# Rows of decays and gates over all partitions: transposing a column read with step 0, in place of a product with a diagonal matrix

## The reference

```python
# branch A, gated DeltaNet, 8 heads, both directions; per chunk, per head
G = cumsum(g)
decay = exp(where(tril, G[:, None] - G[None, :], -inf))
a_low = where(strict, (k*beta) @ k.T * decay, 0)          # unit triangular system
w_v, u_k = triangular_solve(a_low + I, [v*beta, k*beta*exp(G)])
v_new = w_v - u_k @ s
out   = (q*exp(G)) @ s + (q @ k.T * decay) @ v_new
s     = s*exp(G_last) + (k*exp(G_last - G)).T @ v_new

# branch B, mLSTM, 4 heads, both directions; per chunk, per head
d_log = where(tril, b[:, None] - b[None, :] + log_i[None, :], -inf)
m_t   = maximum(b + m, max(d_log, axis=-1))
p_ij  = exp(d_log - m_t[:, None]) * (q @ k.T)
num   = exp(b + m - m_t) * (q @ C) + p_ij @ v             # and den, C, n, m alike
```

## Time and profile before

| | |
|---|---|
| median of 3 runs | 3540.78 us (3540.35 to 3541.26) |
| profiled execution: span, first to last instruction | 3540.6 us |
| instructions profiled | 49,727 |
| TensorE busy | 3332.9 us (94%), 19752 matmul instructions |
| VectorE busy | 2341.5 us (66%) |
| ScalarE busy | 1778.2 us (50%) |
| GpSimd busy | 332.9 us (9%), 333 instructions |
| DeltaNet stage | about 1381 to 1737 us of the span |
| mLSTM stage | about 1737 to 1868 us of the span |

### The profile page before, as it was taken

One profiled execution on the slowest core, in us unless ns is written; L12 is line 12 of the kernel. 1 busy time (PEld: TensorE's weight loads), 2 busy tenths in 40 slices (PEclk: granted clock), 3 DMA queues, 4 the chain that ended last, 5 costly groups with the idle time before them and its releaser, 6 DMA issues. The chain is left out here.

```text
span 3540.6 us, 49727 instructions
## 1 busy us (share of the span) xinstructions
PE 3332.9 (94%) x19752; PEld 2737.8 (77%) x19752; DVE 2341.5 (66%) x2542; ACT 1778.2 (50%) x2276; POOL 332.9 (9%) x333
## 2 busy tenths in 40 slices
PE   5899999999999998999887999977999999999995
PEld 0799998989999998998767998865666666666663
DVE  1578557656665665455576334577888888888886
ACT  2444322333333333555555223445777777777774
POOL 0000000011100002322302100000100100010000
PEclk8999999999999999999998999998999999999997
DMA  9422324545555553112334434678999999999998
GB/s 413 153 93 90 143 108 134 177 165 188 182 175 183 179 171 107 37 49 58 118 85 153 157 109 152 251 274 304 376 390 396 394 379 397 395 376 397 397 376 319
DMA packets 181508, 796.78 MB, mean 225 GB/s; under 512 B 17508, under 2 KB 75236, under 8 KB 102116
## 3 DMA queue, kind: packets, MB, share of 16 engines
q1 hardware_dynamic: 163348, 702.44, 53.7%
q0 software_dynamic: 17136, 86.91, 7.4%
q10 hardware_dynamic: 864, 5.27, 0.4%
HBM read 732.10 MB, written 62.46 MB: 224 GB/s over the span
## 5 line engine op out<-in xcount | busy, mean ns | idle before, releaser
L2510 DVE TENSOR_TENSOR expert_lo<-expert_ring,first_expert_hi 128x2048 fp32r<-128x2048 f32 x288 | 660.1, 2292 | 111.8 <-ACT first_expert_hi L2447 108.0
L2447 ACT ACTIVATE first_expert_hi<-expert_ring 128x2048 fp32r<-128x2048 f32 x285 | 546.9, 1919 | 175.1 <-PE bank L2394 175.1
L2393 PE MATMUL bank<-expert_lo,xeT_hi 128*80 128x512 f32 x1024 | 402.0, 393 | 0.0
L468 PE MATMUL bank<-h_hi,part_hi 128*128 128x320 f32 x960 | 301.4, 314 | 8.2 <-DVE part_lo_x L856 4.5
L2392 PE MATMUL bank<-first_expert_hi,xeT_hi 128*80 128x512 f32 x768 | 303.2, 395 | 1.2 <-DVE xeT_lo L2515 1.2
L2394 PE MATMUL bank<-first_expert_hi,xeT_lo 128*80 128x512 f32 x768 | 299.1, 389 | 0.0
L468 PE MATMUL bank<-h_lo,part_hi 128*128 128x320 f32 x960 | 298.2, 311 | 0.0
L856 DVE TENSOR_TENSOR part_lo_x<-part_x,part_hi 128x1024 fp32r<-128x1024 f32 x120 | 149.4, 1245 | 152.5 <-ACT part_hi L680 145.3
L2510 DVE TENSOR_TENSOR expert_lo<-expert_ring,expert_hi 128x2048 fp32r<-128x2048 f32 x96 | 219.6, 2288 | 43.2 <-ACT expert_hi L2447 43.2
L680 ACT ACTIVATE part_hi<-part_x 128x1024 fp32r<-128x1024 f32 x120 | 127.3, 1061 | 217.2 <-PE bank L468 185.2
L468 PE MATMUL bank<-s_hi,part_hi 128*128 128x320 f32 x720 | 226.7, 315 | 3.7 <-DVE part_lo_x L856 3.7
(11 more groups left out here) (405 smaller groups left out, 7812.6 us busy)
## 6 DMA issues: line engine op xcount, KB each, us to landing
expert_ring<-d_wgate SPq DMA_DIRECT2D x128, 1024.0 KB, 7.0
expert_ring<-d_wup_e SPq DMA_DIRECT2D x128, 1024.0 KB, 7.6
expert_ring<-d_wdown SPq DMA_DIRECT2D x128, 1024.0 KB, 10.4
mod_slot<-d_wmod SPq DMA_DIRECT2D x56, 1024.0 KB, 6.9
part_b<-d_win SPq DMA_DIRECT2D x90, 512.0 KB, 3.7
front_ring<-d_wmod SPq DMA_DIRECT2D x40, 1024.0 KB, 8.0
front_ring<-d_win SPq DMA_DIRECT2D x29, 1024.0 KB, 5.0
d_proj<-out_rows POOLq DMA_DIRECT2D x86, 320.0 KB, 2.4
```

Of the source, the lines that this page charges most:

```text
L468: mm = pe.matmul(part_bank[j][:, 0:HALF_T], w, a[:, kk, :], start=(kk == 0 and x == 0), stop=(kk == HALF_K - 1 and x == 2))
L2393: pe.matmul(out[0:CAP, :], a_hi, lo, start=False, stop=False)
L2447: act.activation(w_hi[n % NSPLIT][:], w[:, n % NSLOT].rearrange("p (k n) -> p k n", n=HALF), ACT.Copy).then_inc(s["we_high"], 1)
L2510: dve.tensor_tensor(w_lo[n % NSPLIT][:], w[:, n % NSLOT].rearrange("p (k n) -> p k n", n=HALF), w_hi[n % NSPLIT][:].bitcast(F32), ALU.subt ...
```

## The change

A new function `rows_of_columns` takes the place of `add_mask` and of the product with ones. For each of the four heads TensorE transposes one column of G, ci or negM, which is read as 128 columns with step 0: a 128x128 operand whose columns are all the same, so that its transpose has the column as a row in every line. The transposition goes through the identity as k's and v's do, in 128 output columns per head. The mask's matmul comes after the four and adds onto them. The diagonal matrices are gone: diagG and diagC from GpSimd, diagM from VectorE, with their semaphores; TensorE now waits in the Mbc fill for negM itself (`nM`, raised by VectorE's drain before exp_neg_m), and in the G and Cbc fills for the bank only. Both hardware loops are written out: all five steps have constant waits and addresses on every engine.

```diff
-def add_mask(pe, k, bank, d):
-    pe.matmul(h4(bank[:]), k.ident_bf[:], all_heads(k.neg_bf[:, d, :]), start=True, stop=False)
+def rows_of_columns(pe, k, bank, columns4, d):
+    for h in range(4):
+        pe.matmul(bank[:, h * P:(h + 1) * P], columns4[:, h:h + 1].to_broadcast([P, P]), k.ident, start=(h == 0),
+                  stop=False, is_transpose=True, skip_group_check=True)
+    return pe.matmul(h4(bank[:]), k.ident_bf[:], all_heads(k.neg_bf[:, d, :]), start=False, stop=True,
+                     skip_group_check=True)
...
         def steps(eng, body):
-            body(0, (0, 0), 0)
-            with eng.Fori(0, TT - 1) as i:
-                body(i + 1, (i + 1, i * -1 + (TT - 1)), 1)
+            for step in range(TT):
+                body(step, (step, (TT - step) % TT), min(step, 1))
...
-                pool.wait_ge(bf, 3)
-                def diagonals(step, tiles, _):
-                    for q, d, h0 in QUADS:
-                        if not isinstance(step, int):
-                            A[q].wait_filled(pool, step + -1, "G")
-                        c = d * 8 + h0
-                        pool.tensor_tensor(dg[q][:], all_heads(k.ident), per_head(col(k.G[:], tiles[d], c, c + 4), P),
-                                           ALU.mult).then_inc(dg_ready[q], 1)
+                def strips_of(step, tiles, _):
                     for n in range(1, len(LEVELS)):
...
                     for q, d, h0 in QUADS:
-                        pe.wait_ge(dg_ready[q], step + 1)
                         A[q].wait_free(pe, step, "G")
-                        add_mask(pe, k, A[q].t, d)
-                        mm = pe.matmul(h4(A[q].t[:]), k.ones, dg[q][:], start=False, stop=True)
-                        mm.then_inc(A[q].filled, 1)
+                        c = d * 8 + h0
+                        rows_of_columns(pe, k, A[q].t, k.G[:, tiles[d], c:c + 4], d).then_inc(A[q].filled, 1)
...
# mLSTM: steps written out in the same way; GpSimd's body with diagC removed
-                        pe.wait_ge(s[d]["dgC"], step + 1)
                         b["D"].wait_free(pe, step, "Cbc")
-                        add_mask(pe, k, b["D"].t, 1 - d)
-                        pe.matmul(h4(b["D"].t[:]), k.ones, dg[d][:], start=False, stop=True).then_inc(b["D"].filled, 1)
+                        rows_of_columns(pe, k, b["D"].t, k.ci[:, tiles[d], 4 * d:4 * d + 4], 1 - d
+                                        ).then_inc(b["D"].filled, 1)
...
-                        pe.wait_ge(s[d]["dgM"], step + 1)
+                        pe.wait_ge(s[d]["nM"], step + 1)
                         b["D"].wait_free(pe, step, "Mbc")
-                        add_mask(pe, k, b["D"].t, d)
-                        pe.matmul(h4(b["D"].t[:]), k.ones, dgM[d][:], start=False, stop=True).then_inc(b["D"].filled, 1)
+                        rows_of_columns(pe, k, b["D"].t, nM[d][:], d).then_inc(b["D"].filled, 1)
...
-                        dve.drain()
+                        dve.drain().then_inc(s[d]["nM"], 1)
                         dve.tensor_scalar(enm[d][:], bM[d][:], -1.0, None, ALU.mult)
-                        dve.tensor_tensor(dgM[d][:], all_heads(k.ident), per_head(nM[d][:], P), ALU.mult
-                                          ).then_inc(s[d]["dgM"], 1)
```

More of the change, by code:

```diff
@@ L1008, in phase_deltanet @@
         staged = [sb(f"dn_staged{d}", [P, 24, P]) for d in range(2)]
-        ktok, vtok, dg, DT, sc = (quads(n) for n in ("ktok", "vtok", "diagG", "decayT", "scoresT"))
+        ktok, vtok, DT, sc = (quads(n) for n in ("ktok", "vtok", "decayT", "scoresT"))
         XT, R, vn, vs = (quads(n) for n in ("XT", "R", "vnew", "vweighted"))
@@ L1022, in phase_deltanet @@
                                                                        "dn_state_out"))
-        dg_ready = [k.sem(f"dg_ready{q}") for q in range(4)]
         QUADS = [(q, q % 2, 4 * (q // 2)) for q in range(4)]
@@ L1102, in diagonals @@
                             cut(pool, p, n).then_inc(strips[p], 1)
-                steps(pool, diagonals)
+                steps(pool, strips_of)
             @block.tensor
@@ L1376, in phase_mlstm @@
         staged2 = [dirs(f"ml_staged{b}_", [P, 16, P]) for b in range(2)]
-        ktok, dg, dgM, ET, PT, kw = (dirs(n, [P, 4, P]) for n in ("ml_ktok", "diagC", "diagM", "expT", "pT", "kweighted"))
+        ktok, ET, PT, kw = (dirs(n, [P, 4, P]) for n in ("ml_ktok", "expT", "pT", "kweighted"))
         vtok = dirs("ml_vtok", [P, 4, DA])
@@ L1387, in phase_mlstm @@
         landed2 = [[k.sem(f"ml_landed{b}_{d}") for d in range(2)] for b in range(2)]
-        sems = ("ready", "dgC", "dgM", "max", "expo", "scalars", "kw", "nu", "den")
+        sems = ("ready", "nM", "max", "expo", "scalars", "kw", "nu", "den")
         s = [{n: k.sem(f"ml_{n}{d}") for n in sems} for d in range(2)]
@@ L1395, in steps @@
         def steps(eng, body):
[L1396 to L1399, removed]
+            for step in range(TT):
+                body(step, (step, (TT - step) % TT), min(step, 1), step % 2, step // 2 + 1)
         def gate(t3, tiles, d, h=None):
@@ L1447, in _ @@
                 pool.drain().then_inc(o_zeroed, 1)
[L1449 to L1455, removed]
             @block.tensor
@@ L1525, in body @@
                         b["A"].wait_filled(act, step, "kT")
-                        if not isinstance(step, int):
-                            act.wait_ge(s[d]["kw"], step)
+                        wait(act, s[d]["kw"], step)
                         act.activation(ktok[d][:], h4(b["A"].t[:]), ACT.Copy).then_inc(b["A"].emptied, 1)
@@ L1536, in body @@
                         b["D"].wait_filled(act, step, "Mbc")
-                        if not isinstance(step, int):
-                            act.wait_ge(s[d]["scalars"], step)
+                        wait(act, s[d]["scalars"], step)
                         act.activation(nMl[d][:].unsqueeze(2), h4(b["D"].t[:])[:, :, END[d]:END[d] + 1], ACT.Copy)
```

## The result

| | before | after |
|---|---|---|
| median, us | 3540.57 (3539.28 to 3541.26, 4 runs) | 3513.36 (3511.10 to 3517.00, 4 runs) |
| ratio, 95% interval | | 0.9920 (0.9908 to 0.9932) |
| profiled execution, span, us | 3540.6 | 3513.6 |

Forecast: 3517.0, range 3510 to 3528. More runs of both in a later comparison gave 3515.38 against 3540.61. The nine executions of the changed kernel lie between 3511.10 and 3517.00 us and their two medians stand 2 us apart, so a difference of 2 us between medians says nothing here.

A forecast was written before the change was run, and what follows sets the result against it. TensorE was taken to bound DeltaNet, and in mLSTM the path through VectorE's pT and back to TensorE. DeltaNet 15.9 plus mLSTM 8.0 made 23.9 us, so 3540.8 became 3516.9, predicted as 3517 us, range 3510 to 3528.

The forecast's parts named there:

- Fill: G fills on TensorE: 0.65 us instead of 1.07, saving 0.42 each, 8.4 us over DeltaNet's 5 steps x 4 quads.
- thin cover: DeltaNet: first KK comes only 0.1 to 0.3 us after ScalarE has emptied its bank, in each step.
- Rival 2: Fills in both stages: step-0 column costs as much as f32 products, so 13.0 us not gained, 3529.9; chance 0.08.
- Written-out steps: DeltaNet steps 1 to 4: VectorE's first strip starts first as in step 0, each stretch 38.40 us, 7.5 us saved.
- DeltaNet: DeltaNet stage, fills and written-out steps together: 15.9 us saved.
- Rival 1: DeltaNet: GpSimd still wins the first strip, in step 0 too; 9.6 us lost, 3526.5; chance 0.13.
- mLSTM: mLSTM path up to pT: 1.73 us saved in steps 1 to 3, 1.45 in step 4, 1.4 in step 0; 8.0.
- Step 0: mLSTM step 0: three fills (1.26) and the diagC wait (0.40), less 0.2 for the clock; 1.4 us saved.
- Rule weighed: TensorE, both stages: the skill's rule that transpositions don't engage full clock would cost each of ten steps clock; forecast rejected it.
- Rival 3: Both stages: clock falls once more per step, after transpositions or waiting for pT; about 15 us, 3532; chance 0.07.
- Rival 4: Both stages: written-out bodies must be fetched, some 10 packets, 40 us if TensorE stood for each, 3557; chance 0.04.

The follow-up runs named there:

- the first of the two versions: Changed kernel with GpSimd's first strips waiting for VectorE's, and mLSTM's four early products with the state ahead of the wait for pT: 3508.33 us, ratio 0.9904.

## Why the prediction was right

- **Fill.** 0.65 forecast, 0.65 measured; from the first G fill to the first KK 1461.01 to 1463.62, 2.61 us, against 4.29 before: 1.68 a step, 8.4 in five. The thin cover held: no KK waits for ScalarE. Rival 2 is out.
- **Written-out steps.** 7.5 forecast; the five stretches sum to 199.46 before and 192.41 after, 7.05. Missing are the 0.57 of step 2. DeltaNet 15.9 forecast, 16.03 measured; 8.4 and 7.05 make only 15.45, and the other 0.58 us, which the sum doesn't have, lie between the stretches and behind the last one (0.38 there), and no run assigns them. So the nearness of 15.9 and 16.03 is in part luck. The cause, one wait fewer in the loop, was argued from 0.02 to 0.06 us in two rows; taking the wait away turned all races. The sum takes the full 2.15 us of steps 2 and 4 and 2.39 of step 1, of which some 1.3 each is a stretch at 1.2 GHz that one execution has in three steps and another, with the same races lost, in two. Rival 1 was right for one step of five.
- **mLSTM.** 8.0 forecast, 8.52 measured, but by two errors that nearly cancel. From the first product with pT to that of step 4 (1755.86 to 1848.20, and 1736.78 to 1821.12) it is 92.34 - 84.34 = 8.00 where 6.64 was forecast (3 x 1.73 + 1.45): at full clock a step saves 1.67, and one stretch at 1.2 GHz fewer gives the rest. The path was read rightly: from M of direction 1 to pT VectorE takes 5.49 us before and 4.67 after (step 1), 0.82 less where 0.89 was forecast, and the other 0.85 lie ahead of it, where the two fills were to give 0.84. Step 0 was to give 1.4 and gave 0.48 (from the first transposition to the first product with pT 12.16 us before, 11.68 after): its granted clock there is 0.77 against 0.87, and VectorE stands 0.44 us at "issue" before M. First before, then after:

```profile
1743.70:1755.86 12.16, 10.79 (x54) 7.81 (x54) 7.30 (x19) 5.70 (x16) 6.05 (x5) 0.87 1.12 283
```

```profile
1725.10:1736.78 11.68, 10.29 (x63) 9.42 (x63) 5.63 (x17) 5.80 (x16) 1.94 (x1) 0.77 1.11 285
```

  The clock rises 3.0 us behind the first transposition in the profile before and 5.4 behind it in the profile after. The change does not decide this: with the new fill it is 2.6 to 3.0 us in three profiles of the study and 5.2 to 6.0 in the others, and with the old fill 7.4 in the one of writing out alone. In the kernel with one wait less on GpSimd it rises after 2.8 us, and the same stretch then takes 10.58 us, 1.58 less than before, near the 1.4 of the forecast:

```profile
1740.43:1751.01 10.58, 9.20 (x62) 8.33 (x62) 5.85 (x17) 5.69 (x16) 2.17 (x1) 0.86 1.13 287
```

  So the term of step 0 was right in kind, and a clock that rose late took about two thirds of it away in the profile after.
- **Rule weighed.** By the rule of "TensorE: Matmul & The Clock Gate" of the Trainium skill, Part 4, that the full clock doesn't engage in transpose mode, each step would have lost clock. The traces disagree: PEclk is 1.00 in all five windows of DeltaNet steps of after, and four transpositions take 0.43 to 0.44 us there. In mLSTM's step 0 of the kernel with one wait less the clock even rises while TensorE, after 7.6 us of idle time, has run nothing but transpositions, from 1740.43 to 1743.2. Rival 3 is out: after has one stretch at 1.2 GHz fewer in mLSTM than before, and none in the DeltaNet steps.
- **Rival 4.** The page counts 119 packets of the instruction queue instead of the 104 of the earlier trace rows, 15 where some 10 were worked out:

```profile
q8 instruction: 119, 1.95, 0.2%
```

  It is 119 too where only TensorE's bodies are written out, so the 15 go with TensorE's code; the other instruction queue, q14, goes from 56 packets to 61 or 62 where the other engines' bodies are written out as well. TensorE does not stand for them: its idle time that ends at "issue" is five times 0.2 us in DeltaNet, one in each step, step 0 too, and none in mLSTM. What is seen are VectorE's 0.44 us in step 2, in all profiles where its DeltaNet body is written out and in none where it is a loop. That fetching causes them is argued, not shown. Rival 4 is out.
- **Total.** The two stages gave 24.55 us where the sum was 23.9; the median is 3.6 us below 3517.0, and 1.6 below it in the second comparison; up to 2.6 us of the lead are no effect of the change. The mechanism and the size of the fill, the race and the path of mLSTM were right. That the two stages meet 23.9 so closely is partly luck, since errors of 0.4 to 1.4 us, the two largest of them from the clock, nearly cancel.

## What to carry to other kernels

A row of a column over all partitions is a transposition of that column read with step 0: four of them cost 0.44 us where the product alone cost 0.86, and the diagonal 1.04 us of GpSimd or 0.69 of VectorE besides. Where VectorE and GpSimd start an operation within 0.1 us of each other, put the one that is waited for first by a semaphore, since one wait more or less decides otherwise. And price a delay that lengthens a standstill of TensorE above its own length, as the clock may fall with it: 0.8 us cost 2.5 a step in the profiled execution here, and only about itself in another one. Before a profile is said to show what brought a stretch at 1.2 GHz, look for the same stretch in the profiles of kernels that are alike in that stage.

## What had not been expected

- VectorE's 128x512 cut took 0.81 us ahead of GpSimd's and 1.92 behind it; GpSimd's 1.31 alone or first and 1.92 second. With both at once the later one pays 0.6 to 1.1 us.
- Standing still for 2.7 to 3.1 us, TensorE kept its clock in two of four mLSTM steps of the changed kernel; with 3.5 to 3.8 us it lost it in all four, with 1.4 to 1.8 (the first of the two versions) in one, with 0.5 to 0.9 in none. Waits of 2.7 to 3.1 us in the kernel with one wait less cost it the clock in none of four. Each of these is one profiled execution.
- A dead VectorE operation of 0.69 us on the path, once a step, cost 7.1 to 9.1 us in the median (3522.48 against 3515.38 and 3513.36); the one of direction 0, partly hidden in a wait, gives 0.22 of the 0.8 us of delay.
